# A third seven-product quad in the first unit of the output projection, and finer releases at the seam to the feed-forward

## What is computed

```python
        x = x + merged @ w_out[l]
        hf = _rms_norm(x, ffn_norm_g[l])
        x = x + (jax.nn.silu(hf @ w_ffn_gate[l]) * (hf @ w_ffn_up[l])) @ w_ffn_down[l]
```

## Time and profile before

| | |
|---|---|
| median of 3 runs | 1621.51 us (1621.15 to 1622.87) |
| the profiled execution | 1620.92 us, of which the span is 1619.1 us |
| busy share of the span | PE 99%, DVE 83%, ACT 57%, POOL 5% |
| first unit of the output projection, 844 to 885 us | VectorE busy for 39.1 of 41 us |

### The profile page before, as it was taken

How to read it: one execution, slowest core, us unless ns; L and a number is a source line. 1 busy time by engine, 2 the same in 40 slices (tenths; PEclk the granted TensorE clock), 3 DMA queues, 4 the chain that set the end, 5 groups by cost and what they waited for, 6 DMA issues and landing times.

```text
span 1619.1 us, 19749 instructions
## 1 busy us (share of the span) xinstructions
PE 1610.6 (99%) x7340; PEld 1333.3 (82%) x7340; DVE 1341.6 (83%) x1399; ACT 924.9 (57%) x1001; POOL 82.1 (5%) x73
## 2 busy tenths in 40 slices
PE   9999999999999999999999999999999999999999
PEld 7888888888888888888888788888888888888887
DVE  5565658898677777777989899999999999999995
ACT  6654555555555544445555665665656655656653
POOL 0000000000011000000000000100100100100101
PEclk9999999999999999999999999999999999999999
DMA  9766555666545555566666746878868868868866
GB/s 355 265 215 193 157 151 177 213 200 198 193 157 167 162 165 171 179 184 205 204 223 201 267 144 217 250 214 254 244 215 246 252 205 251 247 216 241 250 212 178
DMA packets 178013, 341.45 MB, mean 211 GB/s; under 512 B 11792, under 2 KB 16400, under 8 KB 177168
## 3 DMA queue, kind: packets, MB, share of 16 engines
q1 hardware_dynamic: 167056, 319.45, 60.2%
q0 software_dynamic: 10880, 20.97, 7.1%
HBM read 317.31 MB, written 2.10 MB: 197 GB/s over the span
## 4 chain that ended last, share of the span: by engine, by line
PE 81%; issue 14%; DVE 3%; ACT 1%; DMA 1%; POOL 1%; DVEq 0%; ACTq 0%; SPq 0%; POOLq 0%
PE acc L1730 32%; PE at L1821 9%; PE at L1820 9%; PE at L1819 9%; PE acc L1821 5%; PE acc L1819 5%; PE acc L1820 5%; PE at L1730 3%; PE at L1752 2%; POOL rstd L519 1%; DVE w_lo L992 1%; DMA raw<-in_w_ffn_gate 0%; PE at L1799 0%; PE at L1782 0%; DMA raw<-in_w_mem_kv 0%
## 5 line engine op out<-in xcount | busy, mean ns | idle before, releaser
L546 ACT ACTIVATE w_hi<-raw 128x1024 fp32r<-128x1024 f32 x308 | 325.1, 1059 | 318.6 <-PE acc L1730 240.6
L992 DVE TENSOR_TENSOR w_lo<-raw,w_hi 128x1024 fp32r<-128x1024 f32 x308 | 371.9, 1222 | 158.5 <-ACT w_hi L546 153.4
L1730 PE MATMUL acc<-w_hi,hT_hi 128*128 128x512 f32 x664 | 262.9, 396 | 1.2 <-DVEq L1531 1.2
L1730 PE MATMUL acc<-w_hi,hT_lo 128*128 128x512 f32 x664 | 258.8, 390 | 0.0
L1730 PE MATMUL acc<-w_lo,hT_hi 128*128 128x512 f32 x664 | 258.6, 389 | 0.0
L920 ACT ACTIVATE f_hi<-sum 128x2048 fp32r<-128x2048 f32 x60 | 115.2, 1921 | 122.0 <-DVE sum L1608 118.8
L1730 PEld LDWEIGHTS acc<-w_hi,hT_hi 128*128 128x128 f32 x664 | 124.7, 188 | 29.1 <-DVEq L1531 1.6
L1574 DVE TENSOR_TENSOR f_raw_rest<-f_raw,f_hi 128x2048 fp32r<-128x2048 f32 x64 | 145.3, 2284 | 3.7 <-ACT f_hi L910 3.7
L1730 PEld LDWEIGHTS acc<-w_hi,hT_lo 128*128 128x128 f32 x664 | 124.6, 188 | 26.5
L1730 PEld LDWEIGHTS acc<-w_lo,hT_hi 128*128 128x128 f32 x664 | 124.8, 188 | 24.8
L1587 DVE TENSOR_TENSOR sum_rest<-sum,f_hi 128x2048 fp32r<-128x2048 f32 x60 | 137.2, 2287 | 3.9 <-ACT f_hi L920 3.9
(11 more groups left out here) (405 smaller groups left out, 3005.5 us busy)
## 6 DMA issues: line engine op xcount, KB each, us to landing
raw<-in_w_in SPq DMA_DIRECT2D x208, 512.0 KB, 4.0
f_raw<-in_w_ffn_down SPq DMA_DIRECT2D x88, 512.0 KB, 5.0
f_raw<-in_w_ffn_gate SPq DMA_DIRECT2D x80, 512.0 KB, 4.0
f_raw<-in_w_ffn_up SPq DMA_DIRECT2D x80, 512.0 KB, 5.2
proj<-down POOLq DMA_DIRECT2D x40, 512.0 KB, 6.4
raw<-in_w_mem_kv SPq DMA_DIRECT2D x32, 512.0 KB, 5.6
raw<-in_w_out SPq DMA_DIRECT2D x32, 512.0 KB, 4.7
raw<-in_w_o_mem SPq DMA_DIRECT2D x16, 512.0 KB, 5.0
```

What stands on the lines that cost most here:

```text
L546: act.activation(w_hi[:, s % RING], raw[:, s % RING], ACT.Copy).then_inc(hi_done, 1)
L992: v.tensor_tensor(w_lo[:, s % RING], raw[:, s % RING], w_hi[:, s % RING].bitcast(F32), ALU.subtract).then_inc(lo_done, 1)
L1730: e = pe.matmul(dst, a[:, k0 + k, tok], w[:, s % RING, k, :], start=first and k == 0 and n == 0, stop=last and k == 1 and n == 2)
```

## The change

`OUT_KIND` of the first unit becomes that of the second: seven-product quads at positions 3, 5 and 6 instead of 4 and 6. `OUT_K` is reordered so that these positions hold row blocks 1, 2 and 3. acc_free[0] is released after the first instruction of `out_products(1)` and acc_free[1] after the last. The turn of columns 8 to 15 is cut into two: columns 8 to 11 once o_summed is 3, columns 12 to 15 once it is 4.

```diff
-OUT_KIND = ('nnnnSnSn', 'nnnSnSSn')
-OUT_K = ((0, 1, 4, 5, 2, 6, 3, 7), (4, 5, 6, 0, 7, 1, 2, 3))
+OUT_KIND = ('nnnSnSSn', 'nnnSnSSn')
+OUT_K = ((0, 4, 5, 1, 6, 2, 3, 7), (4, 5, 6, 0, 7, 1, 2, 3))
@@ out_products
                 step(v.tensor_tensor(u2, d1, sg[:, 0], ALU.add), block_u2, UNITS_O + unit_rank(r) + 1)
+                if r == 1:
+                    v.nop().then_inc(acc_free[0], 2)
                 v.tensor_tensor(gt[:, 0], d2, u2, ALU.add)
                 step(v.tensor_tensor(sg[:, 1], d3, u2, ALU.add), block_u3, UNITS_O + unit_rank(r) + 1)
                 step(v.tensor_tensor(gt[:, 1], d2, sg[:, 1], ALU.add), block_u, UNITS_O + unit_rank(r) + 1)
+                if r == 1:
+                    v.nop().then_inc(acc_free[1], 2)
@@ VectorE's loop over the 32 steps
                     low_out_combinations()
                 if s % 16 == 14 and "S" in OUT_KIND[s // 16]:
                     out_products(s // 16)
-                    if s == 30:
-                        for p in range(2):
-                            v.nop().then_inc(acc_free[p], 2)
@@ TensorE, first stage of the feed-forward
                 if s == 1:
-                    pe.wait_ge(o_summed, 4)
-                    turn_columns(3 * KD, range(8, KD), proj, 0)
+                    for c in range(2):
+                        pe.wait_ge(o_summed, 3 + c)
+                        turn_columns(3 * KD, range(8 + 4 * c, 12 + 4 * c), proj, 0)
```

## The result

The changed kernel takes 1627.17 us (median of 9 executions, 1626.05 to 1627.37) against 1621.88 us for the kernel before on the same chip: a ratio of 1.0031 with a 95% interval of [1.0022, 1.0039], 5.3 us or 0.3% slower. The profiled execution has a span of 1625.6 us where the earlier trace rows had 1619.1.

A forecast was written before the change was run, and what follows sets the result against it. TensorE's own time was taken as the bound (busy 1610.6 of 1619.1 us). Stall + 4.82, third quad - 0.68 and releases - 0.86 sum to + 3.28 us, 1624.8 on the median; range 1623.7 to 1627.1 and a little over.

The forecast's parts named there:

- the wait alone: Main case: TensorE waits 4.82 us for low_out_combinations at position 3, clock unchanged; 1624.8 us, chance 0.50.
- a unit that lasts other than 4.1 us longer: Sign that the prediction is wrong; it had the output projection's unit end 4.14 us later.
- The clock falls in the gap: Rival: TensorE's clock drops to 1.2 GHz behind the 4.6 us gap, costing up to 2.3 us; 1627.1 us, chance 0.30.
- Third quad on TensorE: Output projection, first unit: a seven-product quad takes 4.76 us where a plain one takes 5.44, so 0.68 us less.
- The place of low_out_combinations: VectorE's queue: low_out_combinations ends at 859.59, TensorE needs it at 854.93 for position 3; stall 4.82 us.
- VectorE holding the unit up further: After the stall VectorE stays 1.2 us ahead at position 6, no further wait; the unit ends 4.14 us later.
- No stall: Rival: low_out_combinations is through by 854.93, so 0.68 and 0.86 us are won; 1620.0 us, chance 0.06.
- The finer releases: Seam after unit 1: the accumulators' wait goes, only eight turns follow the second half of the residual sums; 0.86 us gained.
- The sum: Whole kernel: + 4.82 - 0.68 - 0.86 = + 3.28 us, giving 1624.8 us on the median.

The follow-up runs named there:

- e1: Changed kernel with 18 idle matmuls filling TensorE's standstill before its wait for r_split 10; 1624.72 us, 1.0023 of the kernel before.
- e4: Changed kernel with low_out_combinations one step earlier on VectorE, ahead of low_out_sums(0); 1623.42 us, 1.0016 of the kernel before.
- e9: Changed kernel with ScalarE writing o_whole from PSUM and low_out_combinations moved ahead of low_out_sums(0); 1621.81 us, 1.0001 of the kernel before.
- e10: Changed kernel with the first unit's three seven-product quads at positions 4, 5 and 6; 1624.02 us, 1.0015 of the kernel before.
- e2: Kernel before with the finer releases and cut turns alone, no third quad; 1619.97 us, 0.9994 of the kernel before.
- e7: Kernel before with the earlier release of the accumulators alone, turns in one piece; 1623.09 us, 1.0004 of the kernel before.
- e5: The kernel of e4 with out_whole moved from VectorE to GpSimd; 1625.20 us, 1.0018 of the kernel before.
- e6: Changed kernel with 7 idle matmuls in TensorE's standstill before its wait for r_split 10; 1627.41 us, 1.0030 of the kernel before.

## Why the prediction was right, and where not

**Direction and range** held: the kernel is slower, and 1627.17 lies at the very end of the range, which the prediction lets run from 1623.7 to the clock's 1627.1 and a little over. That the number lies in it is owed to that rival alone. **The case** was not the likeliest one: 1624.8 was forecast for the wait alone at 0.50, and the rival in which the clock falls, 1627.1 at 0.30, is what happened. By the prediction's own sign (a unit that lasts other than 4.1 us longer) its main case was wrong: the units took 6.12 us longer. The step that failed is the chance in "The clock falls in the gap", and with it the sum, which puts the clock at nothing. The chance was argued from gaps of 1.16 and 1.29 us that did no harm, a quarter of the one at hand, while the start of the kernel, the only row after long idling, spoke for it. Its price of 2.3 us at the upper end measured 2.0 to 2.1. By the rule of the Trainium skill's "TensorE: Matmul & The Clock Gate", part 1, that an idle engine falls back to the low clock, this rival was the forecast, and the trace agrees: 0.50 while TensorE stood.

**Third quad on TensorE**, - 0.68: right where the clock holds; e1's quad takes from 859.08 to 863.98 (its last matmul at 863.75, and 0.23 more), 4.9 us with the slow first matmul.

**The place of low_out_combinations**: right to a hundredth. low_out_sums(0) was due at 855.09 and came at 855.53, low_out_combinations at 857.30 and came at 857.73, both the common 0.44 us later. The stall of 4.82 us measured 4.70 between the starts; the slow restart's 0.11 is inside the slow matmuls.

**VectorE holding the unit up further**: right for this kernel (no wait at positions 5 and 6), but only behind the long stall, as e4 shows. Where the clock held behind that stall (e1), the whole term came out: the units took 4.17 us longer, for 4.14 forecast. The "No stall" rival took 0.68 us as won once that wait is gone; e4, e9 and e10 show that VectorE then is the next bound, and that rival's 1620.0 was too low by some 1.7 us (e9).

**The finer releases**, - 0.86: measured - 0.52 here and - 0.71 in e2 (8.63 against 9.34). That the second half of the sums decides, whatever was released before, is what e7 shows. The missing 0.34 us is the sums' own lateness: they began 935.92 - 929.04 - 0.44 = 6.44 us later than before, TensorE was 6.09 later. VectorE had waited longer for the next stage's weights; ScalarE's timeline of the changed kernel reads:

```profile
925.82 1.06 ACT L546 ACTIVATE w_hi<-raw 128x1024 fp32r<-128x1024 f32 x1 [4.23 <-DMA raw<-in_w_ffn_gate]
```

That idle time was 3.90 us in the trace of before. The other six runs with both releases and the turns in their old place (e1, e4, e5, e6, e9, e10) gave 0.57 to 0.80 at the seam. So the term was a little too large throughout, and at least some of the rest goes with the execution: e1 and e6, which have the change whole, stand 0.16 apart.

**The sum**: 4.82 - 0.68 - 0.86 = 3.28 forecast; 4.70 - 0.68 + 2.11 - 0.52 = 5.6 by the rows, 5.3 by the medians; e1, without the clock's part, 4.17 - 0.57 = 3.6 by the rows, 3.9 by the medians.

**Open**: what decides whether a gap of some 2 us lets the clock fall. In the profiled executions 1.90 (e7, with turns behind it) and 2.16 us (e5) did, 2.09 us (e4) did not, and most of e4's other executions have a mean clock under 1.000. The kernel before has such executions too, five to thirteen of 20 to 32 on each chip, 1.0 to 1.3 us longer than the others in the median; where the clock falls in them no trace shows.

## What to carry to other kernels

When a step moves forward, list everything that its first instruction waits for and find each of them in its producer's queue: an operand that was in time for reasons of order is late once other work for the same step is queued ahead of it. Price a standstill of TensorE as long as those that let the clock fall here (1.90 to 4.54 us) with that fall as well, some 2 us. Ask of each wait that is to go what is next behind it on the engine that ends last: here, by the rows, the cut of the turns gave most of the releases' gain, the earlier release of the accumulator nothing by itself, and one more pair of matmuls ahead of the waiting turns gave the most. A change that takes 0.7 us from a full TensorE and puts 4.3 us on a VectorE that is busy for 39 of 41 us found no place to pay here: in no version with the third quad were the units shorter than without it.

## What was not expected of the hardware

The clock fell after a standstill of 2.96 us, and after 1.90 us when turns followed (0.50 in the window, sixteen turns in 2.74 instead of 1.72 us); in e6 it fell only when matmuls had begun again. GpSimd's addition lasted 5.62 us beside VectorE's roundings, where VectorE does it in 2.28, and a VectorE instruction that was issued meanwhile took 4.05 instead of 1.22 us.
